# FFN transition: the last up pair's relus, later additions, squares and stores moved behind the splits of the first down block

## What is computed

```
m = rmsnorm(h, g_mlp)                                  # h: 1024 tokens x 1024
h = h + jnp.square(jax.nn.relu(m @ w_up)) @ w_down     # w_up 1024 x 4096, w_down 4096 x 1024
```

## Time and profile before

| | us |
|---|---|
| median of three executions | 2627.1 |
| lowest and highest | 2626.68, 2628.3 |
| the profiled execution, device time | 2624.4 |
| its span (first to last instruction) | 2622.5 |
| PE busy in the span | 2542.3 (97%) |
| DVE, ACT, POOL busy | 1730.9, 1147.0, 1136.2 |
| stage of pairs 2 to 15, first to last matmul start | 1920.7 to 2191.5 |
| stage of the down blocks 0 to 6, first to last matmul start | 2191.7 to 2471.9 |

### The profile page before, as it was taken

The page is one execution under the profiler, slowest core; times in us unless marked ns, Lnnn a source line. Parts: engine busy times, 40 slices in busy tenths (PEclk is TensorE's granted clock), DMA queues, the critical chain, the costliest instruction groups (busy, mean ns, idle before and its releaser), DMA issues.

```text
span 2622.5 us, 33254 instructions
## 1 busy us (share of the span) xinstructions
PE 2542.3 (97%) x12712; PEld 2022.7 (77%) x12712; DVE 1730.9 (66%) x2061; ACT 1147.0 (44%) x1757; POOL 1136.2 (43%) x1100
## 2 busy tenths in 40 slices
PE   8999999999999999999999999999999998999997
PEld 7877888687787787887676777767888887878886
DVE  7636763677748648658776455565556668999856
ACT  3527882336405305316275545463333334444232
POOL 4633344532342432432441222214645556777652
PEclk9999999999999999999999999999999999999999
DMA  3111002212212112111230001002133333322412
GB/s 140 49 44 33 25 25 86 92 47 101 65 49 81 57 48 73 64 49 61 84 129 25 33 25 33 25 25 97 49 126 107 113 113 121 121 98 104 161 41 81
DMA packets 58137, 189.93 MB, mean 72 GB/s; under 512 B 5952, under 2 KB 6336, under 8 KB 57984
## 3 DMA queue, kind: packets, MB, share of 16 engines
q1 hardware_dynamic: 44704, 143.67, 16.1%
q10 hardware_dynamic: 13280, 44.17, 4.7%
HBM read 158.33 MB, written 29.49 MB: 72 GB/s over the span
## 4 chain that ended last, share of the span: by engine, by line
PE 80%; DVE 11%; ACT 5%; issue 3%; POOL 1%; ACTq 0%; DMA 0%; DVEq 0%; POOLq 0%; SPq 0%
PE PS L991 38%; PE PS L1697 10%; PE PS L1720 8%; PE PS L1321 4%; PE PS L1228 3%; PE PS L1742 2%; PE PS L1554 1%; PE PS L1537 1%; PE PS L1354 1%; PE PS L1127 1%; PE PS L1364 1%; PE PS L1358 1%; PE PS L1141 1%; PE PS L1577 1%; PE PS L1670 1%
## 5 line engine op out<-in xcount | busy, mean ns | idle before, releaser
L839 POOL CAST w_hi<-w_stage 128x1024 fp32r<-128x1024 f32 x130 | 144.4, 1111 | 1046.9 <-PE PS L991 756.9
L842 POOL TENSOR_TENSOR w_lo<-w_stage,w_hi 128x256 fp32r<-128x256 f32 x520 | 494.0, 981 | 10.4
L991 PE MATMUL PS<-XH,w_hi 128*128 128x512 f32 x1216 | 386.6, 399 | 9.0 <-ACT ssd_z L2136 3.3
L991 PE MATMUL PS<-XL,w_hi 128*128 128x512 f32 x1216 | 375.5, 390 | 0.0
L991 PE MATMUL PS<-XH,w_lo 128*128 128x512 f32 x1216 | 375.0, 390 | 0.0
L991 PEld LDWEIGHTS PS<-XH,w_hi 128*128 128x128 f32 x1216 | 221.4, 188 | 65.5 <-issue 12.9
L991 PEld LDWEIGHTS PS<-XL,w_hi 128*128 128x128 f32 x1216 | 228.2, 188 | 48.8
L991 PEld LDWEIGHTS PS<-XH,w_lo 128*128 128x128 f32 x1216 | 228.2, 188 | 48.6
L946 POOL TENSOR_TENSOR w_lo<-w_sums,w_hi 128x256 fp32r<-128x256 f32 x112 | 126.1, 1138 | 59.7 <-ACT w_hi L2482 59.1
L1697 PE MATMUL PS<-ffn_token_sums,w_hi 128*128 128x512 f32 x448 | 138.0, 389 | 0.0
L1720 PE MATMUL PS<-ffn_u_even,w_hi 128*128 128x512 f32 x400 | 125.6, 395 | 5.3 <-DVE ffn_shared L3477 3.2
(11 more groups left out here) (492 smaller groups left out, 6105.1 us busy)
## 6 DMA issues: line engine op xcount, KB each, us to landing
w_stage<-w SPq DMA_DIRECT2D x202, 512.0 KB, 3.3
ssd_sum_rows<-sums_kept ACTq DMA_DIRECT2D x32, 512.0 KB, 3.8
f_kept<-ffn_t SPq DMA_DIRECT2D x32, 512.0 KB, 2.6
ffn_whole_u_even<-f_kept SPq DMA_DIRECT2D x16, 512.0 KB, 4.8
ffn_whole_u_odd<-f_kept SPq DMA_DIRECT2D x12, 512.0 KB, 5.4
H<-x_t ACTq DMA_DIRECT2D x8, 512.0 KB, 8.2
pj_kept<-ple_proj_tiles ACTq DMA_DIRECT2D x8, 512.0 KB, 2.6
h_kept<-H ACTq DMA_DIRECT2D x8, 512.0 KB, 3.6
```

The costliest lines, as they stand in the source:

```text
L839: nc.gpsimd.tensor_copy(w_hi[:, slot, :, :], w_stage[:, slot, :, :]).then_inc(s_w_hi, 1)
L842: nc.gpsimd.tensor_tensor(w_lo[:, slot, k:k + 2, :], w_stage[:, slot, k:k + 2, :], w_hi[:, slot, k:k + 2, :].bitcast(F32), ALU.subtract).t ...
L991: mm = nc.tensor.matmul(outs[:, half, :], wt[:, slot, k, :], a[:, k - first, half * HB:(half + 1) * HB], start=(k == whole[0] and wt is w_ ...
```

## The change

It reorders instructions on DVE, ACT and SP; no instruction is added or removed, and PE and POOL keep their lists.

- DVE: u3 and c22 come straight behind diff 5. Then u_lo 1, diff 6, the weight sums of slab 0, diff 7, diff 4, u_lo 6, 5, 7, **the weight sums of slab 1**, u_lo 2, 3, 4, and only then f(3), f(1), c12, f(8), c21, f(2). The copy at L3477 follows, without the weight sums behind it.
- ACT: the high parts of u come in the order 1, 5, 2, 3, 6, 7, 4, and the four squares of pair 15 stand between the last weight parts of slab 1.
- SP: the two stores of pair 15 stand behind the first weight slab of down block 0's four (d = 2), so the four loads of block 1 and that slab come ahead of them.

```diff
-HIGHS = [(_j, _b) for _b in range(FFN_BLOCKS) for _j in ((1, 5, 6, 7, 2, 3, 4) if _b < DOWN_BLOCKS else (1, 8, 2, 3))]
+HIGHS = [(_j, _b) for _b in range(FFN_BLOCKS) for _j in ((1, 8, 2, 3) if _b == DOWN_BLOCKS else (1, 5, 6, 7, 2, 3, 4) if _b else (1, 5, 2, 3, 6, 7, 4))]
@@ SP
             load(0, 2)
-            store(p, 0)
-            store(p, 1)
             for b in range(DOWN_BLOCKS):
...
                 for s in range(2, 6):
                     next_slab(d0 + 4 * b + s)
+                    if b == 0 and s == 2:
+                        store(p, 0)
+                        store(p, 1)
@@ ACT
                 pair_hi(p, 6)
                 if last:
+                    for j in (2, 3):
+                        u_hi(j, 0)
                     down_hi(0, 0)
                     down_hi(0, 1)
                     u_hi(6, 0)
-                else:
-                    pair_hi(p + 1, 0)
+                    for i in range(2, 6):
+                        down_hi(0, i)
+                    u_hi(7, 0)
+                    u_hi(4, 0)
+                    break
+                pair_hi(p + 1, 0)
                 square_quad(p, "f22")
...
-            square_quad(PAIRS - 1, "f21")
             down_hi(0, 6)
             for d in range(1, 4 * DOWN_BLOCKS):
                 b = d // 4
                 for i in range(7):
                     down_hi(d, i)
+                    if d == 1 and 2 < i:
+                        square_quad(PAIRS - 1, ("f22", "f11", "f12", "f21")[i - 3])
@@ DVE
-                    if i == 0 and ahead:
+                    if i == 0 and d and ahead:
                         weight_sums(*ahead)
...
                 u2(p)
                 if last:
                     diff(5, 0)
-                    u_lo(1, 0)
-                    diff(6, 0)
                 else:
                     pair_sums(p + 1)
                 u3(p)
                 c22(p)
-                f(3, p)
-                f(1, p)
                 if last:
+                    u_lo(1, 0)
+                    diff(6, 0)
                     weight_sums(0, 0)
                     diff(7, 0)
                     diff(4, 0)
+                    for j in (6, 5, 7):
+                        u_lo(j, 0)
+                    weight_sums(0, 1)
+                    for j in (2, 3, 4):
+                        u_lo(j, 0)
+                f(3, p)
+                f(1, p)
                 c12(p)
                 f(8, p)
-                if last:
-                    u_lo(6, 0)
                 c21(p)
                 f(2, p)
-            for j in (5, 7, 2, 3, 4):
-                u_lo(j, 0)
```

More of the change, by code:

```diff
@@ L2514, in _ @@
                     u_hi(6, 0)
-                else:
-                    pair_hi(p + 1, 0)
-                square_quad(p, "f22")
-                if last:
[L2519 to L2522, removed]
-                square_quad(p, "f11")
[L2524 to L2529, removed]
-                square_quad(p, "f12")
[L2531 to L2535, removed]
-            square_quad(PAIRS - 1, "f21")
+                    for i in range(2, 6):
[4 more added lines that the diff above has]
+                pair_hi(p + 1, 0)
+                square_quad(p, "f22")
+                pair_hi(p + 1, 1)
+                square_quad(p, "f11")
+                pair_hi(p + 1, 2)
+                square_quad(p, "f12")
+                pair_hi(p + 1, 3)
             down_hi(0, 6)
```

## The result

The changed kernel takes 2631.35 us (median of 20 executions, 2628.61 to 2633.87) against 2625.9 us for the kernel before (median of 20, 2623.18 to 2631.5). The ratio is 1.0018, with a 95% interval of 1.0011 to 1.0025: slower by 4.7 us (2.9 to 6.6); the two medians themselves lie 5.45 us apart, inside that interval. The forecast was 2632.9 us, slower by 5.8 us. The profiled execution has a span of 2628.8 us (before: 2622.5).

What follows compares the result with a forecast made beforehand. It took DVE's list up to the copy, which releases PE, as the bound at the seam: 1.18 + 1.47 + 2.40 + 0.75 = +5.8 us, so 2632.9 us, range 2629.2 to 2635.5.

Steps and rivals of the forecast that it cites:

- The question is when the copy comes: Seam between the stages: PE's restart follows DVE's copy at L3477 by 0.14 us, so the copy's place decides, not the splits'.
- low clock: Term (d), PE after the copy: slow matmuls cost 2.5 us after a 12 us stop instead of 1.75, +0.75 us.
- the edge that I had named: Whole kernel: a difference under about 0.2% (5.25 us) can hardly be told from no change; the forecast was 0.22%.
- the 2205 that I had named as the sign of being wrong: DVE's copy was forecast near 2206.58; a start before 2205 would show the prediction wrong.
- the wait for POOL and its block: On DVE, slab 1's weight sums wait for POOL's seventh split of slab 0, 2.05 us.
- meetings with slab 1's splits: Before the copy, POOL's second to fourth splits meet u_lo 2, 3, 4 (3 x 0.54) and the fifth meets f(8) (0.55).
- term (c): DVE's SBUF operations and POOL's splits go one after the other; meetings and wait 7.4 us before the copy, +2.40 us.
- meetings stay as many as now: Rival, chance 0.26: no added DVE-POOL meetings, only (a), (b) and (d), +3.4 us, 2630.5 us.
- faster: Rival, chance 0.05: DVE's 5.0 us of meetings with POOL vanish, -2.35 us, 2624.8 us.
- worse: Rival, chance 0.17: slab 0's last splits come a microsecond later, low clock lasts through slab 1; about +8, 2635.2 us.
- term (a): On DVE before u3: free at 2178.44 while u3 cannot start until 2179.62; idle time +1.18 us.
- Costed at nothing: ACT's and SP's reorder (high parts, squares, block 1's loads, stores) was taken to cost nothing, being covered by later need.

Runs made afterwards that it cites:

- experiment 2: The changed kernel with the weight sums of slab 1 back behind the copy; ratio to the kernel before 1.0004.
- experiment 5: The changed kernel with one more wait on ACT, holding POOL's second and later splits of slab 1 until the copy; ratio to the kernel before 1.0017.
- experiment 3: The changed kernel with the copy and three additions of slab 0 among the last low parts, slab 1's weight sums behind these; ratio to the kernel before 0.999.
- experiment 4: As experiment 3, with the three PSUM reads f(1), c12, c21 before the relus f(3), f(8), f(2); ratio to the kernel before 0.9991.
- experiment 7: As experiment 4, with three relus in block 1's first slab, squares in its second, stores behind its last weight slab; 2621.9 us, ratio to the kernel before 0.9985.
- Experiment 6: The changed kernel with u_lo 1 put back between diff 5 and u3, into DVE's idle time; ratio to the kernel before 1.0021.
- experiment 1: The changed kernel again, with no edit; ratio to the kernel before 1.0017.

## Why the prediction was right

**The bound.** "The question is when the copy comes" held. PE's long stop ends 0.14 us after the copy in both kernels, and in experiments 2 and 5 block 1 moved with the copy: copy -3.86 and block 1 -3.9 us, copy -1.93 and block 1 -2.4 us (the rest is the low clock: products 2, 3 and 4 took 6.36 in place of 6.89 us). Where the copy no longer came last (3, 4, 7), the next wait that the code has, c21, took its place. The front of the seam did become 4.2 us faster as worked out (13.33 in place of 17.52 us), and in the changed kernel it was worth nothing, as the copy came later all the same. The size fell to the near side of the edge that I had named: 0.18% measured where I had 0.22%, and I had given slower by over 0.2% somewhat more weight (0.57) than within (0.41). The interval leaves both open. Two things make the agreement look better or safer than it is. The profiled span, 2628.8 us where 2628.3 was forecast, holds the 1.52 us that lie before the changed stretch, and that is luck. And the copy, 2207.47 on the clock of its own profile, is at 2205.95 when counted from the u2 of the kernel before: 0.6 us below the forecast of 2206.58, and a microsecond above the 2205 that I had named as the sign of being wrong.

**The terms**, forecast and measured:

| term | forecast | measured | where |
|---|---|---|---|
| idle time before u3 | +1.18 | 1.22 | changed, L3357 |
| weight sums of slab 1, own time | +1.47 | 1.5 | changed, L3443 to L3448 |
| the wait for POOL and its block | 2.05 | 1.8 | 1.39 and 0.45, L3443 |
| meetings with slab 1's splits | 2.2 | 1.93 | experiment 5 |
| term (c), all meetings and that wait, less those before | +2.40 | +1.8 | 6.9 less 5.0 |
| copy, in sum | +5.05 | +4.42 | 31.77 less 27.35 |
| low clock | +0.75 | +1.06 | 6.89 less 5.83 us for products 2, 3, 4 |
| slab 1 | +5.8 | +5.48 | 39.48 less 34.00 |

The row of term (c) comes from the list as a whole. From diff 5 to the copy DVE took 28.84 us; less 1.30 us from the end of diff 5's step to u3, and 20.7 us that the instructions take alone, 6.9 us are left for meetings and the wait. With diff 5 itself 0.19 us earlier behind u2 than before, 1.30 + 1.47 + 1.84 - 0.19 gives the +4.42 us.

The term that was mis-sized is (c), by some 0.6 us: u_lo 1 lost 0.3 us and slab 0's sums 0.4 us to POOL, where I had 0.53 and 0.6, and the wait was 0.2 us shorter. In these rows a meeting costs its full half microsecond where POOL's split waits behind an operation of DVE and starts with its end; a split that is already running when DVE's operation comes is partly over. The difference was in part made up by the low clock, which cost 0.3 us more than taken. The rival "meetings stay as many as now" (+3.4 us) is out, since experiment 5 takes the new meetings away and the copy comes 1.9 us earlier. Of the other two, "faster" needed meetings of under 2.35 us in all, where 6.9 were measured, and "worse" a low clock through slab 1, where the granted clock was 0.98 from 2214 to 2216, as slab 1 began.

One step of mine was not sound, though its sum was nearly right: term (a) as a loss by itself. Experiment 6 shows that filling the idle time gives back 0.26 us, not 1.2, so most of it is only the other face of a meeting that the kernel before had (2.21 us for u_lo 1) and the changed one had not. In the sum the two were counted with opposite signs, which is why it came out.

**Costed at nothing.** For ACT's and SP's reorder no cost shows: in the changed kernel PE waits for neither at the seam, and with both as in the changed kernel, experiments 3 and 4 reach block 1 earlier than the kernel before. ACT did wait 1.36 us for a load in front of u_hi 2, which the working had not; slab 0's first high part of weights came at 9.05 us from u2 in place of the 8.1 worked out, and PE did not wait for it. The stores went out at 2212 us and the next weight slab 2.9 us behind. In the 50 us after the seam ACT waits once for a weight slab to land, 1.5 us, as it did before for 1.1 us; PE has no wait there in either kernel.

**The low clock**: the cost of a restart did not simply grow with the stop. After stops of 3.25, 7.84, 9.62 and 11.66 us products 2, 3 and 4 took 5.83, 6.80, 6.36 and 6.89 us, and after the stops of 11.67 and 11.68 us of experiments 1 and 6 they took 6.68 us. The long stops all cost more than the short one, but not in the order of their length, and one and the same stop differed by 0.2 us. One row could not have given the size. That the 2.5 us taken from the span's start came near (2.81 and 2.60 measured) is in part luck: there the matmuls step at 0.43 us while the trace gives a granted clock of 1.00, so that row is read by its pace alone. The Trainium skill, "TensorE: Matmul & The Clock Gate", section "What's actually happening", says that the number of slow matmuls of one kernel varies from run to run with where its start falls; these six restarts do not contradict it.

## What to carry to other kernels

Ask which instruction releases the engine that bounds the kernel, and count only what stands in front of that one in its queue: here a reorder made the first half of a seam 4.2 us faster and the kernel 5 us slower, because the releasing copy kept its place at the end of a list that grew. Work moved ahead of the releasing instruction brings with it what it waits for and what it sets off on other engines: here 1.5 us of sums cost 3.9. Moving the release itself, and putting work that nobody waits for (the relus and stores of values read 200 us later) where the queue has slack, gave 4.6 us by the profiles (3.9 us by the ratio of 0.9985) in place of a loss.

## What the runs showed of the hardware that I had not expected

DVE's idle time beside POOL was not lost time here. A 128x512 split of POOL that a low part of u meets costs DVE 1.0 us (2.21 against 1.22 us for the same operation); an idle DVE lets it pass for nothing, so filling 1.2 us of idle time with such an operation gained 0.26 us. In the same way DVE's operations with a PSUM input, put between those with both inputs in SBUF, seem to have given POOL its turns: in experiment 3 u_lo 2, 3 and 4 took 1.21 to 1.25 us each with two additions or one between them, where in experiment 2 the same low parts, in a row with the same splits of POOL pending, took about 1.7.
